# Regrouping the modulation units between the q, k products of a hybrid decoder layer

## The reference, cut to what matters

```python
mod = (silu(c) @ w_ada + b_ada).reshape(bsz, 6, 1, D_MODEL)     # sh1, sc1, gt1, sh2, sc2, gt2
hn = rmsnorm(x, g_norm1) * (1.0 + sc1) + sh1
q, k, v, xl, gl = split(hn @ w_in)                              # q, k, v: 8 heads x 128 columns each
q, k = rmsnorm(q, g_q), rmsnorm(k, g_k)                         # per head
z = q @ k.T * SB_SCALE + bias                                   # scores of a head
lm = where(mask, log_sigmoid(-z), 0);  rc = reversed_cumsum(lm)
attn = where(mask, exp(log_sigmoid(z) + rc - lm), 0) @ v        # stick-breaking attention
lru = rglru(conv(xl)) * gelu(gl)
x = x + gt1 * (concat(attn, lru) @ w_out)
hn2 = rmsnorm(x, g_norm2) * (1.0 + sc2) + sh2
x = x + gt2 * ((gelu(ug) * uv) @ w_down)                        # ug, uv: conv(hn2 @ w_up)
```

## Time and profile before

| | us |
|---|---|
| median of 3 runs | 2878.15 (2876.41 to 2879.63) |
| the profiled execution | 2877.52 |
| its span, from first to last instruction | 2876.0 |
| TensorE busy in the span | 2801.0 (97%) |
| VectorE, ScalarE, GpSimd busy | 1766.9, 1185.2, 312.8 |
| mean granted TensorE clock | 0.993 |

### The profile page before, as it was taken

How to read it: one execution, slowest core, us unless ns; L and a number is a source line. 1 busy time by engine, 2 the same in 40 slices (tenths; PEclk the granted TensorE clock), 3 DMA queues, 4 the chain that set the end, 5 groups by cost and what they waited for, 6 DMA issues and landing times.

```text
span 2876.0 us, 61999 instructions
## 1 busy us (share of the span) xinstructions
PE 2801.0 (97%) x24651; PEld 2687.5 (93%) x24651; DVE 1766.9 (61%) x2755; ACT 1185.2 (41%) x1450; POOL 312.8 (11%) x591
## 2 busy tenths in 40 slices
PE   6999999999999999799999999999999999999999
PEld 4889999878888999699999999999999999999999
DVE  3434334545454323988888888888888655555553
ACT  3345444544544222644444444444444422222222
POOL 0011110112221000111111111111111000000000
PEclk9999999999999999899999999999999999999999
DMA  9997775566665866533333333333333633333323
GB/s 363 354 335 240 248 265 184 171 222 230 223 220 186 265 209 199 173 117 109 107 100 118 102 112 100 114 104 114 100 109 104 212 110 110 107 107 107 107 86 108
DMA packets 512730, 478.16 MB, mean 166 GB/s; under 512 B 15593, under 2 KB 426079, under 8 KB 510189
## 3 DMA queue, kind: packets, MB, share of 16 engines
q1 hardware_dynamic: 487298, 363.97, 40.1%
q0 software_dynamic: 24224, 111.42, 11.2%
q10 hardware_dynamic: 1044, 0.43, 0.1%
HBM read 441.69 MB, written 67.62 MB: 177 GB/s over the span
## 4 chain that ended last, share of the span: by engine, by line
PE 90%; DVE 4%; DMA 3%; ACT 2%; issue 1%; SPq 0%; DVEq 0%; ACTq 0%; POOLq 0%
PE ps L826 44%; PE ps L1299 37%; PE ps L840 2%; PE ps L1127 1%; DMA wide_act<-in_w_ada_dram 1%; PE ps L1093 1%; PE ps L1078 1%; DMA xr<-in_w_ada_dram 1%; PE ps L929 1%; DMA raw<-in_w_in_dram 1%; PE ps L1082 1%; PE ps L993 1%; PE ps L959 0%; DMA keys_r<-key_save 0%; PE ps L971 0%
## 5 line engine op out<-in xcount | busy, mean ns | idle before, releaser
L1299 PE MATMUL ps<-ops,w_hi 128*128 128x288 f32 x4608 | 919.5, 296 | 1.0 <-DVE w_lo L2363 1.0
L1299 PEld LDWEIGHTS ps<-ops,w_hi 128*128 128x128 f32 x4608 | 740.0, 189 | 1.4 <-DVE w_lo L2363 1.4
L1299 PE MATMUL ps<-ops,w_lo 128*128 128x288 f32 x2304 | 678.7, 295 | 0.0
L1952 DVE TENSOR_TENSOR w_lo<-raw,w_hi 128x1024 fp32r<-128x1024 f32 x240 | 293.2, 1225 | 562.5 <-ACT w_hi L1411 562.4
L826 PE MATMUL ps<-gs,w_hi 128*128 128x288 f32 x3072 | 607.1, 294 | 0.0
L826 PE MATMUL ps<-act_hi,w_hi 128*128 128x288 f32 x1792 | 544.9, 304 | 3.9 <-DVE act_lo L1998 1.1
L826 PE MATMUL ps<-act_lo,w_hi 128*128 128x288 f32 x1792 | 528.7, 295 | 0.0
L826 PE MATMUL ps<-act_hi,w_lo 128*128 128x288 f32 x1792 | 527.9, 295 | 0.0
L1411 ACT ACTIVATE w_hi<-raw 128x1024 fp32r<-128x1024 f32 x240 | 253.4, 1058 | 662.6 <-PE ps L826 645.4
L826 PEld LDWEIGHTS ps<-gs,w_hi 128*128 128x128 f32 x3072 | 490.4, 188 | 0.0
L826 PE MATMUL ps<-gs,w_lo 128*128 128x288 f32 x1536 | 451.2, 294 | 0.0
(11 more groups left out here) (374 smaller groups left out, 3125.6 us busy)
## 6 DMA issues: line engine op xcount, KB each, us to landing
raw<-in_w_up_dram SPq DMA_DIRECT2D x120, 512.0 KB, 4.2
raw<-in_w_down_dram SPq DMA_DIRECT2D x128, 384.0 KB, 3.2
raw<-in_w_in_dram SPq DMA_DIRECT2D x80, 512.0 KB, 5.7
ada_q<-in_w_ada_dram SPq DMA_DIRECT2D x64, 512.0 KB, 6.0
key_save<-in_cache_k_dram POOLq DMA_DIRECT2D x64, 512.0 KB, 5.4
page<-in_cache_v_dram POOLq DMA_DIRECT2D x64, 512.0 KB, 4.6
keys_r<-key_save POOLq DMA_DIRECT2D x52, 512.0 KB, 5.1
ax<-in_w_up_dram SPq DMA_DIRECT2D x48, 512.0 KB, 4.8
```

The lines of the kernel that those rows point to most:

```text
L1299: mm = pe.matmul(ps[:, bank, 0:HALF], w[slot][:, kk, :], moving(i, kk, low), start=i not in ADDED and kk == 0 and w is w_hi and not low, s ...
L1952: dve.tensor_tensor(w_lo[s][:], raw[s][:], w_hi[s][:].bitcast(F32), ALU.subtract).then_inc(lo_done, 1)
```

## The change

In the loop of TensorE's `qkv`, for heads 2 to 8, a product and a unit change places twice. Unit 4 i now stands behind product k = 1, directly before unit 4 i + 1; and unit 4 i + 2 behind product k = 3, directly before unit 4 i + 3.

```diff
                 turn_mod([mod_rows_q[:, 2, :]], 4, 7 + i, 0)
+                product(u, 1, gps[0], act_hi, act_lo, first=False, k0=KB)
                 ada_unit(ada_q, n, low_q)
-                product(u, 1, gps[0], act_hi, act_lo, first=False, k0=KB)
                 ada_unit(ada_q, n + 1, low_q, end=True)
                 pe.wait_ge(sem("mod_taken"), 8 + i)
                 scores(i)
                 wait(pe, sem("rq_taken"), i)
                 product(u, 2, gps[1], act_hi, act_lo, last=False)
+                product(u, 3, gps[1], act_hi, act_lo, first=False, k0=KB)
                 ada_unit(ada_q, n + 2, low_k)
-                product(u, 3, gps[1], act_hi, act_lo, first=False, k0=KB)
                 ada_unit(ada_q, n + 3, low_k, end=True)
                 sums(i)
```

## The result

The changed kernel takes 2885.68 us (median of 7 runs, 2884.93 to 2892.89) against 2878.15 (7 runs, 2875.1 to 2883.18) before. The ratio is 1.0033, with a 95% interval of 1.0024 to 1.0042. That is 9.5 us slower by the ratio (6.9 to 12.1), 7.5 by the two medians. 2885.0 was forecast, with a range of 2874 to 2889.5. The profiled execution took 2886.76 us, its span is 2885.2; before it was 2877.52 and 2876.0.

What follows compares the result with a forecast made beforehand. TensorE was taken to bound 90% of the chain, with head 2 waiting on loads. Head 2's loss 10.4, clock 0.3, later heads' gain 3.8 gave +6.9 us: 2885.0 against the median 2878.15, range 2874 to 2889.5.

Steps and rivals of the forecast that it cites:

- part 2: Head 2: block 11 issued 6.4 us later, landing at 168.0, sums starting at 184.35; loses 10.4 us.
- Later heads: Heads 3 to 8: TensorE saves 0.63 us a head by the new order, 3.8 us in six heads.
- first pair: Heads 3 to 8, transpose's end to scores, product k = 1 before two units: 0.32 us saved a head.
- second pair: Heads 3 to 8, scores' end to sums, two products then two units: 0.31 us saved a head.
- about even: Heads 3 to 8: later unit loads, 7 us more at worst, still about even with 15.5 us available; costed at nothing.
- rival 3: Unit loads of heads 3 to 8 come late; 1 us a head would add 6 us, 2891; chance 0.08.
- The clock: Head 2, behind the longer wait: slower granted clock adds 0.3 us, bounds -1.6 and 1.5.
- Rival 1: Head 2's loads don't matter, block 11 landing before 157.6; 3.8 us gained, 2874.3; chance 0.12.
- Rival 2: Head 2: queues share evenly, block 11 lands at 163.3; +2.2 us, 2880.3, no measurable change; chance 0.18.

Runs made afterwards that it cites:

- e15: Also called after again: the changed kernel unaltered, profiled a second time; 2891.4 us (one run).
- e2: Changed kernel with the units paired in head 2 only, old order in heads 3 to 8; 2889.75 us, 1.0049 of the kernel before.
- e4: Changed kernel with GpSimd's key copies in head 2 held until ten blocks are used, SP's order kept; 2878.22 us, 1.0007 of before.
- e11: Changed kernel with only the pair of units behind product k = 1, in heads 2 to 8; 2889.44 us (one run).
- e14: Changed kernel with only the pair of units behind product k = 3, in heads 2 to 8; 2873.28 us (one run).
- e13: Changed kernel with blocks 11 and 12 ahead of unit 6, first eight key copies held, VectorE taking scores before block k = 5's low part; 2869.16 us, 0.9974.
- e3: Changed kernel with blocks 11 and 12 issued ahead of units 6 and 7 on SP; 2873.25 us, 0.9986 of the kernel before.
- e1: Changed kernel with head 2 in its old order and units paired in heads 3 to 8 only; 2873.1 us, 0.9990 of before.
- e10: The kernel before, unaltered, profiled a second time; 2876.61 us (one run).

## Why the prediction was right

**The mechanism.** Each step of part 2 is in the changed profile, at the place where it was looked for: unit 6 issued at 152.12 (152.3 forecast), block 11 at 153.42 (153.3), landed at 168.17 (168.0), sums at 184.56 (184.35). The distance from landing to sums, worked out as 16.35 us, measured 16.39 or 16.40 in the five profiles in which block 11 bound: after, after again, e2, e4 and e11 (there it landed at 168.66 and the sums began at 185.06). ScalarE sat idle for 13.6 us before its `hi` of block 11 (some 12 forecast). e4 and e11 with e14 show its two causes by taking each away: the unit behind the product, which delays the issue, and the copies, which lengthen the transfer.

**Later heads.** 3.8 us were forecast and 3.44 measured (2.86 + 0.58). The first pair was right (0.32 forecast, 0.34 in e11). The second pair is the mis-sized term: 0.24 instead of 0.31 (e14), and the missing part is a short wait for the softplus that a view of waits before could not show, since TensorE was the later of the two. With that wait gone, in e13, a head gains 0.68 where 0.63 was forecast. The loads cost nothing, as said: the 44 unit halves there landed like this (compare):

```profile
DMA to landing us min/median/max: 3.7/6.6/10.9
```

The last halves were in some 5 us before their use, so "about even" was too dark, and rival 3 did not come.

**The clock.** The sums with the next product took 189.91 + 6.74 - 184.56 = 12.09 us; 10.93 before. That is 1.2 instead of 0.3, inside the bounds. Windows of the changed kernel (us, busy us of PE, PEld, DVE, ACT and POOL with counts, then the granted clock, DMA share and GB/s):

```profile
171.50:184.50 13.00, 1.04 (x20) 0.55 (x16) 7.38 (x12) 8.92 (x9) 0.00 (x0) 0.57 1.06 386
184.60:190.40 5.80, 5.80 (x23) 5.61 (x24) 1.50 (x2) 1.76 (x3) 0.00 (x0) 0.50 0.98 305
190.50:194.00 3.50, 3.50 (x29) 3.50 (x28) 1.97 (x7) 1.27 (x1) 0.00 (x0) 1.00 0.30 116
```

While TensorE was nearly idle, the clock fell to 1.2 GHz, and it stayed there for the first 5.9 us of work. Before, the sums began at the full clock, and the 3.4 us at 1.2 GHz began 1.3 us later. The 0.3 had no row under it, and the cost doesn't grow with the wait. The five profiles in which block 11 bound, all of them with the first pair in head 2, show this:

| | wait for the sums, us | at 1.2 GHz from the sums' start, us | sums and next product, us |
|---|---|---|---|
| e4 | 5.3 | 5.5 | 11.88 |
| e11 | 9.8 | 4.8 | 11.57 |
| after | 10.3 | 5.9 | 12.09 |
| e2 | 10.6 | 3.7 | 11.03 |
| e15 | 12.7 | 3.6 | 11.00 |

So the term was between 0.07 and 1.16 against the 10.93 of before, and the longest wait had the smallest. Why the clock rises sooner in one execution than in another is left open.

**Unit 7.** The 2.7 us wait on `ada_q` was not forecast. It costs nothing, as it lies inside the wait for the sums, but e3 shows that it is next in line. It is also why TensorE waited 10.3 us for the sums where over 12 were forecast: with the 2.7 it is 13.0.

**The sum.** Forecast +10.4 + 0.3 - 3.8 = +6.9. Measured, by the same terms, +10.6 + 1.15 - 3.44 = +8.3, and +9.2 in the whole span with what the paged keys and later stages add. By the medians it is 7.5, by the ratio 9.5. That 2885.0 stands so close to 2885.68 is partly luck: the landing of block 11 moved by 3.2 us between two executions, and the kernel before was itself profiled with a wait on block 12 of 2.3 us, which was 0.5 the second time and in e1. From head 2's transpose to that of head 3 it is 56.70 us in the first profile of before, but 53.34 in e10 and 53.30 in e1; the changed kernel has 68.65 and 70.41. So the loss of head 2 is 12 to 17 us, depending on which two profiles are compared, and the forecast's 10.7 (10.4 + 0.3) was read against the one profile of before that had the wait and the slow clock. Less the 3.4 us of the later heads, 8.5 to 13.6 us are left, and the 7.5 to 9.5 that the times show lie at the lower end of it.

**The rivals.** Rival 1 needed a landing before 157.6 and got 168.17. That no block took under 7.7 us holds for blocks 11 to 13 alone: the last block before block 10, issued at 127.76, landed 4.4 us later, when neither `x_save` nor the copies were under way. Rival 1 was still out of reach: with the copies held back block 11 took 6.64 us and landed at 159.14 (e4). Rival 2, an even share of the queues, put the landing at 163.3. The DMA queues from 154 to 164 us of the changed kernel (packets, MB, share), against the earlier trace rows:

```profile
q0 software_dynamic: 165, 2.62, 68.2%
q1 hardware_dynamic: 551, 1.00, 29.1%
```

and from 164 to 170 us, against the earlier trace rows:

```profile
q1 hardware_dynamic: 1353, 1.20, 67.3%
```

In the first ten us SP's queue moved 1.00 MB, more than the 0.72 that the forecast used and less than the 1.7 of an even share. With the changed kernel's own 1.00 and 1.20 MB the forecast's way of adding up gives a landing at 166.9, so that its 168.0 was met to 0.2 us is luck too. The Trainium skill says in DMA: Bandwidth & Descriptors, section Queues, rings and completion order, that the queues take turns a packet at a time; with packets of unlike size that need not be an even share of bytes, and the trace shows that it is not (by its own count of packets, 551 with 1.00 MB against 165 with 2.62). So the rule alone does not speak for rival 2, as the prediction had it; the turns themselves no run here shows.

## What to carry to other kernels

Before an instruction is moved behind another, look up which semaphore it raises, who waits for that, and what stands behind the waiter in its queue: here a unit moved by 6.4 us delayed a weight block that has nothing to do with it. The price of a late load is its later issue plus what it then collides with, and the second part was the larger (8.5 to 11.3 us against 2.3 to 4.1). Where the transfers of a stage collide, one profile shows one draw; take a second of the kernel before, too, before a term is read from it. Where a kernel's every iteration is bound by one engine but the first is not, treat the first apart, and give both their own order.

## What the runs showed of the hardware

- A 512 KB block issued by SP behind the two halves of a unit took 14.1 to 18.0 us beside key copies of 512 KB each, six of them issued within 6.1 us (e11, e2, after, e15), and 6.64 us when the copies were held back (e4).
- The issue itself can stop the issuer: SP needed 10.01 us to put two unit halves in its queue (the changed kernel, from 154.22), and 0.76 us for the block just before.
- After waits of 5.3 to 12.7 us the granted clock was at 1.2 GHz when the work began, and it was back at 2.4 GHz 3.6 to 5.9 us later; the longest wait had the shortest of these times. The sums with the next product then took 11.00 to 12.09 us, against 9.33 at full clock.
